# HGRN2 stage of a two-layer model: level operands made one level ahead, gate projections in eight pieces, weight differences moved

## The reference

```python
def hgrn2_mixer(h, w_in, lb, norm_w, w_out):
    proj = h @ w_in
    q = silu(proj[q part]); f = proj[f part]; i = proj[value part]; g = proj[gate part]
    f_t = lb + (1 - lb) * sigmoid(f)
    log_f = log(max(f_t, 1e-30));  k = (1 - lb) * sigmoid(-f)
    o = hgrn2_chunkwise(q, k, log_f, i)          # 8 heads of width 128
    o = head_rmsnorm(o, norm_w) * silu(g)
    return o @ w_out
```

## Time and profile before

| | us |
|---|---|
| median of 3 runs | 1935.07 |
| lowest, highest run | 1929.24, 1937.03 |
| the profiled execution, its own time | 1934.42 |
| its span in the trace | 1932.5 |

### The profile page before, as it was taken

How to read it: one execution, slowest core, us unless ns; L and a number is a source line. 1 busy time by engine, 2 the same in 40 slices (tenths; PEclk the granted TensorE clock), 3 DMA queues, 4 the chain that set the end, 5 groups by cost and what they waited for, 6 DMA issues and landing times. The chain is left out here.

```text
span 1932.5 us, 36862 instructions
## 1 busy us (share of the span) xinstructions
PE 1893.2 (98%) x15078; PEld 1629.3 (84%) x15078; DVE 912.4 (47%) x1225; ACT 578.6 (30%) x1234; POOL 727.9 (38%) x624
## 2 busy tenths in 40 slices
PE   9999999999999999999999999999999999999997
PEld 8778745888887888888877887778999999999996
DVE  3898687677565455444436777765100000000023
ACT  1443213455533111110036657543120211111102
POOL 5755522565544434444526777651300000000011
PEclk9999999999999999999999999999999999999999
DMA  9213750222215666631212111201957578778893
GB/s 332 91 55 142 266 206 25 81 98 88 83 44 198 212 205 214 217 121 60 103 66 67 67 56 61 74 13 70 322 207 248 197 233 276 256 262 334 336 348 155
DMA packets 82824, 313.58 MB, mean 162 GB/s; under 512 B 10121, under 2 KB 10641, under 8 KB 82529
## 3 DMA queue, kind: packets, MB, share of 16 engines
q1 hardware_dynamic: 75952, 289.73, 42.5%
q0 software_dynamic: 4464, 14.35, 2.1%
q10 hardware_dynamic: 2241, 7.14, 1.0%
HBM read 301.43 MB, written 9.75 MB: 161 GB/s over the span
## 5 line engine op out<-in xcount | busy, mean ns | idle before, releaser
L261 PE MATMUL banks<-sb_act,sb_ring 128*64 128x112 f32 (+9 forms) x5088 | 620.9, 300 | 1.2 <-ACT sb_ring L468 0.7
L261 PEld LDWEIGHTS banks<-sb_act,sb_ring 128*128 128x128 f32 (+1 forms) x5088 | 592.4, 174 | 23.2 <-issue 4.5
L261 PE MATMUL banks<-sb_x_norm,sb_ring 128*128 128x256 f32 (+3 forms) x1616 | 330.9, 403 | 3.4 <-ACT sb_ring L468 2.3
L261 PEld LDWEIGHTS banks<-sb_x_norm,sb_ring 128*128 128x128 f32 (+1 forms) x1616 | 242.4, 171 | 66.3 <-issue 29.6
L3730 DVE TENSOR_TENSOR sb_act<-sb_work,banks 128x192 f32<-128x192 f32 (+7 forms) x88 | 27.2, 309 | 482.7 <-PE banks L261 475.4
L443 POOL TENSOR_TENSOR sb_ring<-sb_ring 128x512 f32<-128x512 f32 x146 | 206.7, 1415 | 104.2 <-PE banks L261 53.7
L261 PE MATMUL banks<-sb_work,sb_ring 128*64 128x256 f32 (+2 forms) x1124 | 231.6, 407 | 3.2 <-ACT sb_ring L468 2.1
L261 PEld LDWEIGHTS banks<-sb_work,sb_ring 128*128 128x128 f32 (+1 forms) x1124 | 155.9, 165 | 56.9 <-issue 34.6
L3261 POOL DMA_INDIRECT sb_work<-first_expert_rows,sb_table x8 | 7.5, 939 | 442.9 <-DMA first_expert_rows<-sb_x_norm 440.8
L3532 ACT ACTIVATE sb_work<-banks 128x192 f32<-128x192 f32 (+7 forms) x88 | 25.8, 294 | 295.2 <-PE banks L261 293.2
L2370 ACT ACTIVATE sb_work<-banks 128x256 f32<-128x256 f32 x84 | 32.3, 384 | 216.8 <-PE banks L261 216.8
(11 more groups left out here) (530 smaller groups left out, 2589.2 us busy)
## 6 DMA issues: line engine op xcount, KB each, us to landing
sb_ring<-in_w_moe_up SPq DMA_DIRECT2D x176, 512.0 KB, 4.7
sb_ring<-in_w_moe_down SPq DMA_DIRECT2D x64, 704.0 KB, 6.5
sb_act<-in_cond_w SPq DMA_DIRECT2D x84, 512.0 KB, 3.7
sb_ring<-in_w_ffn_up SPq DMA_DIRECT2D x44, 512.0 KB, 5.1
sb_ring<-in_w_h_in SPq DMA_DIRECT2D x32, 512.0 KB, 4.3
sb_ring<-in_w_in SPq DMA_DIRECT2D x28, 512.0 KB, 6.2
sb_ring<-in_w_m_in SPq DMA_DIRECT2D x24, 512.0 KB, 4.0
sb_ring<-in_w_ffn_down SPq DMA_DIRECT2D x16, 704.0 KB, 5.4
```

Source lines behind the costliest of these rows:

```text
L261: last = m.nc.tensor.matmul(out[part], weights[:, part], act, start=start, stop=stop, skip_group_check=skip)
```

## The change

Three things change, all in `stage_h`.

- **Operands one level ahead.** VectorE does `times(h, j + 1)` at level j, right behind the take of level j - 1 and the adds, instead of at the start of j + 1, for j = 3 and 4 in heads 1 to 6 and for j = 1 to 4 in head 7.
- **Pieces.** g6 is made in four pieces of 3, 3, 1 and 1 steps before levels (6, 4) to (6, 7), g7 in four of 2 steps before (7, 0) to (7, 3). ScalarE takes g6 at (6, 7) and g7 at (7, 3), each behind its other work of that level; the square of head 5's values is no longer ahead of two decays.
- **Differences.** GpSimd's weight differences start one level later, have two in head 6 and six in head 7, and eight behind the loop; the wait for heads 0 to 5 (`head_out`) moves behind the loop, and its wait for all projection blocks is gone.

```diff
--- before.py
+++ after.py
@@ -2567,8 +2567,10 @@
 H_PAIRS = [(("f", 2), ("q", 1)), (("v", 0), ("v", 1)), (("f", 3), ("q", 2)), (("v", 2), ("v", 3)), (("f", 4), ("q", 3)),
            (("g", 1), ("g", 2)), (("f", 5), ("q", 4)), (("v", 4), ("v", 5)), (("f", 6), ("q", 5)), (("g", 3), ("g", 4)),
            (("f", 7), ("q", 6)), (("v", 6), ("v", 7)), (("g", 5), ("q", 7))]
-H_LAST = {(6, 5): ("g", 6), (7, 2): ("g", 7)}
-H_BLOCKS = H_FIRST + [block for pair in H_PAIRS for block in pair] + list(H_LAST.values())
+H_LAST = {(6, 4): ("g", 6, 0, 3), (6, 5): ("g", 6, 3, 6), (6, 6): ("g", 6, 6, 7), (6, 7): ("g", 6, 7, 8),
+          (7, 0): ("g", 7, 0, 2), (7, 1): ("g", 7, 2, 4), (7, 2): ("g", 7, 4, 6), (7, 3): ("g", 7, 6, 8)}
+H_TAKEN = {(6, 7): ("g", 6), (7, 3): ("g", 7)}
+H_BLOCKS = H_FIRST + [block for pair in H_PAIRS for block in pair] + list(H_TAKEN.values())
 H_BESIDE = [[2, 2, 2, 1, 2, 2, 2, 1]] * 6 + [[2, 2, 2, 1, 0, 0, 0, 0], [0] * 8]
 
 
@@ -2631,9 +2633,9 @@
     wide = lambda t: t.rearrange("p (k c) -> p k c", c=P)
     tail = lambda q, i: m.ring[:, rows(q, HK), D + i * P:D + (i + 1) * P]
     shared = lambda bank: ps[:, bank, :].rearrange("p (a c) -> p a c", c=HALF)
-    MADE_6 = {4: (0, T1), 5: (0, T3), 6: (1, T1), 7: (1, T3)}
-    MADE_7 = {1: (0, T2), 2: (1, T2), 3: (0, T4), 4: (1, T4), 5: (2, T1), 6: (2, T3), 7: (3, T1)}
-    MADE = [(3, T3), (2, T2), (3, T2), (2, T4), (3, T4)]
+    MADE_6 = {5: (0, T1), 7: (0, T3)}
+    MADE_7 = {1: (1, T1), 3: (1, T3), 4: (0, T2), 5: (1, T2), 6: (0, T4), 7: (1, T4)}
+    MADE = [(2, T1), (2, T3), (3, T1), (3, T3), (2, T2), (3, T2), (2, T4), (3, T4)]
     quads = Quads(m, out, heads, pairs.sums,
                   lambda q: (shared(0), shared(1), shared(7)) if q == 0 else (ps[:, 2:4, LO], shared(4), shared(6)),
                   [(wide(A[:, 8, :]), wide(A[:, 9, :]), wide(A[:, 12, :])),
@@ -2663,6 +2665,17 @@
                     return
                 make = by_feature if b > 1 else by_features(m, m.HN, KD, norm.need(m, pe))
                 make(ps[:, b % 2, :], m.ring[:, s, :]).then_inc(m.blocks_done, 1)
+
+            def project_part(kind, h, first, last):
+                b = at[kind, h]
+                if first == 0:
+                    plan.wait_loaded(m, pe, b)
+                    pe.wait_ge(m.evac, plan.done + b - 1)
+                for k in range(first, last):
+                    made = in_strips(m, ps[:, b % 2, :], m.ring[:, plan.slot(b), rows(k, P)], m.HN[:, k, :], k == 0,
+                                     k == KD - 1)
+                if last == KD:
+                    made.then_inc(m.blocks_done, 1)
 
             def values(h):
 
@@ -2696,7 +2709,7 @@
                     n = h * LEVELS + j
                     pairs.multiply(pe, H_BESIDE[h][j])
                     if (h, j) in H_LAST:
-                        project(*H_LAST[h, j])
+                        project_part(*H_LAST[h, j])
                     if h == HEADS - 1 and j == 4:
                         pe.wait_ge(head_out, 2 * EARLY)
                         pe.wait_ge(m.evac, plan.done + plan.n)
@@ -2878,28 +2891,27 @@
                 ahead(h, 2)
                 edges(h)
                 keep(h, 2)
-                if (h, 2) in H_LAST:
-                    take(*H_LAST[h, 2])
-                    load_exponentials()
                 ahead(h, 3)
                 if 0 < h < HEADS - 1:
                     logs(h + 1)
                 keep(h, 3)
+                if (h, 3) in H_TAKEN:
+                    take(*H_TAKEN[h, 3])
+                    load_exponentials()
                 keep(h, 4)
                 ahead(h, 4)
                 if h == HEADS - 1:
                     quads.keep(act, 0, OF_1)
                 keep(h, 5)
-                if (h, 5) in H_LAST:
-                    norms[h - 1].square(m, act)
-                    take(*H_LAST[h, 5])
-                    load_exponentials()
                 ahead(h, 5)
                 keep(h, 6)
-                if h and (h, 5) not in H_LAST:
+                if h:
                     norms[h - 1].square(m, act)
                 ahead(h, 6)
                 keep(h, 7)
+                if (h, 7) in H_TAKEN:
+                    take(*H_TAKEN[h, 7])
+                    load_exponentials()
             take_cross(HEADS - 1)
             quads.keep(act, 0, OF_7)
             norms[HEADS - 2].root(m, act, False)
@@ -2960,12 +2972,10 @@
                     combine(h, j - 1)
                     if h == HEADS - 2 and j in MADE_6:
                         quads.combine(pool, *MADE_6[j])
-                    if h == HEADS - 1:
-                        if j == 5:
-                            pool.wait_ge(head_out, 2 * EARLY)
-                            pool.wait_ge(m.blocks_done, plan.done + plan.n)
+                    if h == HEADS - 1 and j in MADE_7:
                         quads.combine(pool, *MADE_7[j])
                 combine(h, LEVELS - 1)
+            pool.wait_ge(head_out, 2 * EARLY)
             for made in MADE:
                 quads.combine(pool, *made)
             for k in range(KD - 1):
@@ -3045,6 +3055,7 @@
             inputs(S4)
             sums(0)
             forget(1)
+            ahead_of = lambda h: () if h == 0 else (3, 4) if h < HEADS - 1 else (1, 2, 3, 4)
             for h in range(HEADS):
                 q, k = q_of(h), k_of(h)
                 times(h, 1)
@@ -3057,9 +3068,12 @@
                 finishes = 1 if h == HEADS - 1 else 3
                 for j in range(1, LEVELS):
                     if j > 1:
-                        times(h, j)
+                        if j - 1 not in ahead_of(h):
+                            times(h, j)
                         take(h, j - 1)
                         add(h, j - 1)
+                    if j in ahead_of(h):
+                        times(h, j + 1)
                     if 0 < h < HEADS - 1 and j == 3:
                         sums(h + 1)
                     if h > 1 and finishes <= j <= finishes + 1:
```

## The result

The changed kernel is slower: 1941.99 us, median of 15 runs (1937.76 to 1944.63), against 1933.35 us for the kernel before in the same sessions (15 runs, 1929.24 to 1937.03). The ratio is 1.0043, 95% interval 1.0036 to 1.0049. I had forecast 1930.4 and a range up to 1938.0.

The account below looks back on a forecast made before the run. TensorE, busy 1893.2 of 1932.5 us, was taken as the bound, with 9.6 us of idle time to win. Gains of 2.0 and 2.7 us took 1934.42 to 1929.7, plus 0.65 for the median: 1930.4 us; range 1923.5 to 1938.

Parts of the forecast that it names:

- part 1: Heads 2 to 5: the 0.69 us wait ahead of level 5 goes, some 0.2 comes back; gain 2.0 us.
- Rival 2: Heads 2 to 5: a moved VectorE product takes 0.95 us more beside GpSimd; each head loses 0.42; median 1934.1; chance 0.2.
- The clock: Half clock at the seam to the next stage may be met differently: plus or minus 3 us, an uncertainty, not a term.
- Part 2: Head 6: no wait ahead of level (6, 4), but TensorE waits 2.0 us at the products of pairs.
- Part 3: Seam to head 7: level (7, 3) starts 2.9 us earlier after a 1.7 us wait; gain 2.7 us.
- Part 4: GpSimd's weight differences, eight behind the loop: zero cost, with a cover of 5 us.
- Part 5: Table loads of g7 and loads of the last weights: zero; at most 1.9 us if the g7 cover of 0.8 goes.
- Rival 3: Take of g6: ScalarE's queue becomes the bound and the kernel gets slower, 1936.7 us; chance 0.1.
- four signs: No new pair-products wait; heads 2 to 5 `times` 1 us or more; root after 1263; TensorE waiting for GpSimd behind the loop.
- the first sign for a right one: TensorE's waits from 1040 to 1334 us sum to about 5 instead of 9.6 us.

Follow-up runs that it names:

- e6_hold: The changed kernel with two GpSimd instructions held back in heads 2 to 6, about as the order of before held them: 1929.65 us, ratio 0.9983.
- e3_diffs: The kernel before with only the GpSimd weight differences moved: 1934.57 us, ratio 1.0006.
- e9_level5_only: The changed kernel with only the times of level 5 ahead in heads 1 to 6, head 7 as changed: 1941.77 us, ratio 1.0048.

## Why the prediction was wrong

**The step that failed is in part 1**: "They ended at about 1216.54 and now end one `times` later, 0.46, at 1217.0". I took over every duration of VectorE from the old order, and with it, unsaid, the old order of GpSimd beside it. Measured from the start of level 3, the fourth product ended after 10.8 us and now ends after 13.1: 2.3 later and not 0.46. With GpSimd held in about its old order (`e6_hold`) it ends after 11.5, so 1.6 us of the 2.3 come from GpSimd's new order. The gain forecast for heads 2 to 5 was 2.0 us; the stretch up to the values of head 5 lost 10.7.

That `e6_hold` came out at 1929.65, within 1 us of my 1930.4, is in part luck. I had started from a median of three runs, 1935.07; beside `e6_hold` the kernel before ran at 1933.13, so the gain is 3.3 us by the ratio and not 4.7. Nor do its parts fit: by the traces, cut as in the table, heads 2 to 5 win 0.7 us and not 2.0, the stretch to (7, 3) wins 3.2 (2.7), 2.3 are lost behind it and 1.0 is won at the seam. Holding GpSimd turns the sign; it doesn't show that the sum was right.

**Rival 2 had the mechanism, but too small and with a wrong argument against it.** "The blocked time is set by GpSimd's instructions, which are no more than before" holds for the kernel, not for the stretch from the take to the products of pairs: there it is five instructions where it was three. I priced one blocked `times` at 0.95; it lost 0.49 itself, and the two products behind it another 0.94. The Trainium skill, "SBUF — State Buffer", Summary: rules for kernel authors, says that of two such instructions, one of VectorE with two SBUF inputs and one of GpSimd that reads SBUF, the second is blocked until the first is through. The trace agrees in kind: `times` and the two products on 384 columns, all with two SBUF inputs, are the ones that stretch (0.43 to 0.92, 0.97 to 1.51, 0.56 to 0.96).

**The clock** was the second error. I read that a wait of 2.94 us had left it at 1.00 and concluded that waits of this size are safe, so that it got no term inside the stage. Waits of 2.0 us cost 1.7 us more each, three times in heads 2 to 5 and once in head 7. No rival had this: 6.8 us in the stage, beside 5.4 us of added waits in heads 2 to 5. The fall of 3.4 us at the seam stayed away in return, so that the net cost is 3.4.

**Part 2** held: a wait of 0.49 for the bank (0.34 in my sum), none ahead of (6, 4), and 1.6 us at the products of pairs (2.0). **Part 3** held up to level (7, 3): the root ended at 1272.2, 7.2 us behind g6's last piece (start of its take 1265.01), as the 7.3 said; the wait was 1.98 (1.7), and the lead since the values of head 5 2.7 us (2.9). VectorE waited for the root as foreseen. Then a fall of the clock took 1.7 of the lead back. The table load was 1.28 with no drain behind it here too. **Part 4** was priced at zero and has the 0.8 us wait ahead of the last norm; `e3_diffs` shows that it comes with the moved differences. How, was not tried. GpSimd itself was never waited for behind the loop, as I had it. **Part 5** held. **Rival 3** (ScalarE's queue) was not it: undoing only the moved `times` removes the loss with that queue in place.

Of the four signs that I named for a wrong prediction none was quite there, which is a fault of the signs: `times` of level 5 took 0.92 us in each of heads 2 to 5 and the sign asked for 1, and the root came later than 1263 only because everything did. What told was the first sign for a right one: 13 us of waits in all instead of 5.

## What to carry to other kernels

An instruction that is moved earlier releases whoever waits for it. Before costing such a move, look up what the released engine does next and what that runs beside; an accidental wait may have been keeping two engines apart. If the result of a queue is needed in a fixed place, it is worth as much to move the place: the early operands alone cost about 9 us (ratio 1.0045), the later place alone was worth nothing, and the changed kernel with the later place was 7 us faster than the one before. And a wait of TensorE of 2 us is to be costed with a possible fall of the clock, here 3.7 us instead of 2.

## What was not expected of the hardware

- The granted clock does not go by the length of a wait alone. It stayed at full behind 2.94 and 2.91 us (kernel before) and behind 2.08 and 2.22 us (head 2 of the changed kernel and of `e9_level5_only`), and fell to half behind 2.04, 2.08, 2.05 and 1.98 us in the changed kernel. So with 2.08 us it stayed in head 2 and fell in head 4 of the same execution. The fall at the seam to the next stage is in the trace before and not in the changed one. What decides was not settled.
- A fall cost 1.7 us of work each time; the one at the seam to the next stage 1.7 in some of these kernels and 3.4 in others.
- In the same kernels the running sum (L2990 before, L3000 changed) took 2.19 us in head 5 before and 1.64 in the changed one: what one instruction loses to its neighbour another wins. Sums over a queue say more than single rows.
